# A transformer kernel on one core: output projection by token tiles, with the next norm's first tile transposed inside it

## What is computed

```python
for l in range(DEPTH):                                   # DEPTH = 2
    x = x + 0.5 * swiglu_ffn(rms_norm(x, ffn1_norm[l]), ffn1_w_in[l], ffn1_w_out[l])
    h = rms_norm(x, mix_norm[l])
    ...                                                  # three mixers y_a, y_b, y_c and gates g from h @ w_in
    merged = (g[:, :, 0] * (y_a @ w_branch[l, 0])
              + g[:, :, 1] * (y_b @ w_branch[l, 1])
              + g[:, :, 2] * (y_c @ w_branch[l, 2]))
    x = x + merged @ w_out[l]                            # the output projection, 256x1024 by 1024x1024
    x = x + 0.5 * swiglu_ffn(rms_norm(x, ffn2_norm[l]), ffn2_w_in[l], ffn2_w_out[l])
```

## Time and profile before

| | |
|---|---|
| time, median of 3 runs | 1829.95 us (1828.91 to 1839.23) |
| the profiled execution's own time | 1829.92 us |
| its span in the profile | 1828.1 us |
| mean granted clock of PE | 0.992 |
| busy share: PE, DVE, ACT, POOL | 98%, 57%, 45%, 4% |
| chain that ended last: PE, DVE, ACT, DMA | 90%, 4%, 3%, 2% |

### The profile page before, as it was taken

The page is one execution under the profiler, slowest core; times in us unless marked ns, Lnnn a source line. Parts: engine busy times, 40 slices in busy tenths (PEclk is TensorE's granted clock), DMA queues, the critical chain, the costliest instruction groups (busy, mean ns, idle before and its releaser), DMA issues.

```text
span 1828.1 us, 27099 instructions
## 1 busy us (share of the span) xinstructions
PE 1789.1 (98%) x11448; PEld 1584.1 (87%) x11448; DVE 1046.3 (57%) x1226; ACT 818.6 (45%) x885; POOL 77.6 (4%) x145
## 2 busy tenths in 40 slices
PE   8999999999999999999999999999999999999998
PEld 8998797877999899987978779998887976889996
DVE  4555356887655455553669876455666534545553
ACT  4554345552654445543555526544123123535542
POOL 0000000000000000000000001000561100000000
PEclk9999999999999999999999999999999999999999
DMA  7537255444655645372555446855254223436371
GB/s 253 184 125 282 81 165 160 156 148 138 207 180 192 213 151 184 120 286 81 165 164 159 141 138 208 186 196 207 92 162 79 72 90 115 139 122 213 126 276 58
DMA packets 194332, 293.15 MB, mean 160 GB/s; under 512 B 9298, under 2 KB 128884, under 8 KB 194244
## 3 DMA queue, kind: packets, MB, share of 16 engines
q1 hardware_dynamic: 191988, 287.72, 46.6%
q0 software_dynamic: 1936, 4.14, 2.1%
q10 hardware_dynamic: 320, 0.01, 0.0%
HBM read 289.49 MB, written 2.36 MB: 160 GB/s over the span
## 4 chain that ended last, share of the span: by engine, by line
PE 90%; DVE 4%; ACT 3%; DMA 2%; issue 1%; ACTq 0%; DVEq 0%; SPq 0%
PE acc L225 22%; PE acc L226 22%; PE acc L227 22%; PE acc L271 3%; PE acc L194 2%; PE acc L206 2%; PE acc L3030 2%; PE acc L462 1%; DMA ring<-in_ffn_w_in 1%; PE acc L2725 1%; PE acc L253 1%; PE acc L1304 1%; ACT big L1432 1%; ACT part_hi L216 1%; PE turn L1409 1%
## 5 line engine op out<-in xcount | busy, mean ns | idle before, releaser
L430 DVE TENSOR_TENSOR w_lo<-ring,w_hi 128x2048 fp32r<-128x2048 f32 x160 | 361.9, 2290 | 211.4 <-ACT w_hi L426 211.3
L225 PE MATMUL acc<-xT_hi,w_hi 128*128 128x256 f32 x1680 | 476.0, 283 | 1.2 <-DVE w_lo L430 0.8
L227 PE MATMUL acc<-xT_hi,w_lo 128*128 128x256 f32 x1680 | 475.4, 283 | 0.0
L226 PE MATMUL acc<-xT_lo,w_hi 128*128 128x256 f32 x1680 | 475.4, 283 | 0.0
L426 ACT ACTIVATE w_hi<-ring 128x2048 fp32r<-128x2048 f32 x160 | 301.3, 1912 | 150.1 <-PE acc L227 99.6
L225 PEld LDWEIGHTS acc<-xT_hi,w_hi 128*128 128x128 f32 x1680 | 322.5, 192 | 1.7 <-DVE w_lo L430 1.0
L226 PEld LDWEIGHTS acc<-xT_lo,w_hi 128*128 128x128 f32 x1680 | 322.5, 192 | 0.0
L227 PEld LDWEIGHTS acc<-xT_hi,w_lo 128*128 128x128 f32 x1680 | 322.5, 192 | 0.0
L225 PE MATMUL acc<-w_hi,hT_hi 128*128 128x512 f32 x440 | 172.3, 392 | 0.0
L227 PE MATMUL acc<-w_hi,hT_lo 128*128 128x512 f32 x440 | 171.3, 389 | 0.0
L226 PE MATMUL acc<-w_lo,hT_hi 128*128 128x512 f32 x440 | 171.3, 389 | 0.0
(11 more groups left out here) (550 smaller groups left out, 2978.7 us busy)
## 6 DMA issues: line engine op xcount, KB each, us to landing
ring<-in_ffn_w_in SPq DMA_DIRECT2D x88, 1024.0 KB, 6.1
ring<-in_w_in SPq DMA_DIRECT2D x52, 1024.0 KB, 5.0
ring<-in_ffn_w_out SPq DMA_DIRECT2D x44, 1024.0 KB, 6.4
ring<-in_w_branch SPq DMA_DIRECT2D x12, 1024.0 KB, 5.1
ring<-in_w_out SPq DMA_DIRECT2D x12, 1024.0 KB, 4.9
ring<-in_w_gate SPq DMA_DIRECT2D x11, 1024.0 KB, 5.2
ring<-in_w_up SPq DMA_DIRECT2D x11, 1024.0 KB, 6.8
ring<-in_w_down SPq DMA_DIRECT2D x11, 1024.0 KB, 6.0
```

The source lines that it names most:

```text
L225: pe.matmul(o, a_hi, wh, start=start, stop=False)
L226: pe.matmul(o, a_hi, wl, start=False, stop=False)
L227: return pe.matmul(o, a_lo, wh, start=False, stop=stop)
L430: vec.tensor_tensor(w_part(w_lo, r), raw_part(c0, r), w_part(w_hi, r).bitcast(F32), ALU.subtract).then_inc(f.lo, 1)
```

## The change

The projection's loops are exchanged: for each token tile m, for each half n, its two chunks. Tile 0 is so complete after half of the blocks. `tail.vec` of tile 1 is waited for once, ahead of its first block. Ahead of the last half (m = 1, n = 1), PE transposes tile 0 of the next norm (n2), which `first_gate` then leaves out (`turned=True`). DVE handles the transposed tile 0 before it waits for tile 1 (`late` is left out). Chunk 12 is split sooner: on ACT between the two tiles of merged, on DVE ahead of tile 1 of merged. Chunk 13 is split last as before. The chunks in the ring and the order of the loads are the same.

```diff
-        def ffn_pe(pe, f, n, c0, G0, between, asides={}):
+        def ffn_pe(pe, f, n, c0, G0, between, asides={}, turned=False):
...
-                norm_pe(pe, n, tiles=(0,))
+                if not turned:
+                    norm_pe(pe, n, tiles=(0,))
                 wait_chunk(pe, c0)
...
                 last_branch_pe(pe)
-                for n in range(2):
-                    for m in range(MT):
-                        pe.wait_ge(tail.vec, 6 + 2 * m)
+                for m in range(MT):
+                    pe.wait_ge(tail.vec, 6 + 2 * m)
+                    for n in range(2):
+                        if m == 1 and n == 1:
+                            norm_pe(pe, n2, tiles=(0,))
                         for i in range(2):
                             if n == 0 and m == 0 and i == 1:
                                 merged_pe(pe, 1)
...
                 merged_in_act(act, 0)
+                tail_part_act(act, 12)
                 merged_in_act(act, 1)
-                tail_part_act(act, 12, 13)
+                tail_part_act(act, 13)
...
                 last_branch_vec(vec, 1, 1)
-                tail_part_vec(vec, 11)
+                tail_part_vec(vec, 11, 12)
                 merged_vec(vec, 1)
                 merged_in_vec(vec, 1)
-                tail_part_vec(vec, 12, 13)
+                tail_part_vec(vec, 13)
...
                 add_norm_vec(vec, lambda e, m: add_tile_to_x(e, m, C_WO + 3, G_WO, 1.0, 3 * l + 2), n2, col[:, R["ffn2"]:R["ffn2"] + 8],
-                             late=True, between=lambda e: first_split_vec(e, f2, C_FFN2))
+                             between=lambda e: first_split_vec(e, f2, C_FFN2))
...
-                ffn_pe(pe, f2, n2, C_FFN2, G_FFN2, lambda e: None, asides={4: params2_pe, 6: s5_c_pe} if l == DEPTH - 1 else {})
+                ffn_pe(pe, f2, n2, C_FFN2, G_FFN2, lambda e: None, asides={4: params2_pe, 6: s5_c_pe} if l == DEPTH - 1 else {}, turned=True)
```

## The result

The changed kernel takes 1846.88 us (median of 12 runs, 1835.85 to 1855.51) against 1835.54 us before (12 runs, 1828.91 to 1843.73). The ratio is 1.0066, 95% interval 1.0046 to 1.0086: slower by 0.66% (11.3 us between the medians), within the 1% of the forecast's "same", but above its range and more than its 7.3 us. The profiled execution took 1841.32 us, span 1839.5 us, 11.4 us over that of before.

The account below looks back on a forecast made before the run. PE, busy 98% of the span, was taken as the bound. Per layer 2.66 + 0.99 - 0.18 + 0.17 = 3.64 us, 7.3 us for two layers on 1829.92, gave 1837.2 us; range 1831.5 to 1843.5.

Parts of the forecast that it names:

- Wait for chunk 13: At the projection's fourth block PE waits 2.38 us for this split; with a slower first matmul, +2.66 us a layer.
- Transposes in the stream: Tile 0's eight transposes, moved inside the projection, add 0.99 us a layer to PE's stream.
- The gap behind T: PE's 2.06 us wait after the projection's last block (end T) moves behind the first FFN product; only 0.18 us gained.
- FFN's chunk 1: In the second FFN, its later load and waiting ACT copy delay tile 1's square by 0.17 us (0 to 1.1).
- Chunks 12 and 0 and tile 0's transposes: Projection and FFN: all in time, costing nothing; chunk 12 by 0.9 us, chunk 0 with three blocks, transposes with 0.4 us cover.
- rival (a): PE's clock falls to half in the projection's and FFN's new waits, one to four times: 1839 to 1844 us; chance 0.28.
- (b): No wait for chunk 13 at the projection's fourth block: only 0.98 us a layer lost, 1831.9 us; chance 0.12.
- (c): Gap before the FFN really removed: 1.07 us a layer gained, 1827.8 us with no wait for chunk 13; chance 0.05.
- The 0.96 for "within 1%": Whole kernel: chance 0.96 that the time stays within 1% of before, neither faster nor slower by more.

Follow-up runs that it names:

- experiment 3: Changed kernel with the next norm's tile 0 transposed behind the last block again, leaving loop exchange and sooner chunk 12 split; ratio 1.0049 to the kernel before.
- experiment 1: Changed kernel with chunk 13 split sooner on ACT and DVE; ratio 1.0023 to the kernel before.
- experiment 2: Changed kernel with both new waits kept but filled with throwaway matmuls, five and four; ratio 1.0039 to the kernel before.
- Experiment 4: Changed kernel with chunk 13 split sooner and the second wait covered by 4 us of products ahead of tile 1's transposes; ratio 0.9989 to the kernel before.
- 5 to 8: Experiment 3 with chunk 13 sooner, 1.0009; experiment 1, second wait filled, 1.0009; kernel before, three old waits filled, 0.9979; Experiment 4, those three filled, 0.9984.

## Why the prediction was wrong

**The terms of the sum.** Wait for chunk 13: forecast 2.38 us of waiting and 2.66 in all; the changed kernel waited 2.38, experiment 3 has 2.66 and 2.64. The chain behind it (DVE two splits, copy of merged tile 1, ACT, DVE) was as told, step by step. Transposes in the stream: forecast 0.99, measured 0.94 and 1.00 (experiment 1). The gap behind T: forecast that it moves behind the first product and gives 0.18 back; B is 10.54 in experiment 2 against 10.55, so it moved and gave nothing back. Tile 1's transposes began 3.90 us behind T', the number forecast; what I had as 4.08 before was read from the chain, while the same instructions began at 466.65 = T + 3.92 by PE's own list, so the 0.18 was not there. FFN's chunk 1: forecast 0.17 of delay. It landed 5.1 us after its issue, and its copy was done at 465.78, 0.8 us before tile 1's square could start (0.7 in layer 1); nothing. Sum: forecast 3.64 a layer, measured 3.52 and 3.51 (experiment 2). Chunks 12 and 0 and tile 0's transposes were in time and cost nothing.

**The step that failed** is the one at which rival (a) was kept out of the forecast: the falls of PE's clock behind "two waits of 2.4 and 1.9 us into each layer, between these sizes" stand in the sum with nothing, and (a) got 0.28. I read the waits of 2.1 and 3.2 us as special, because transposes or long pauses stood around them, and took the 2.06 us gap behind T as the nearest row. But that gap has transposes in it and only 1.2 us of idle PE, and the row that I named for it shows the clock within the gap and not behind it (it is 1.00 there too). Both new waits, 2.4 and 2.2 us of nothing, are nearer to the other rows. Two more waits of the kernel before, of just these lengths, I left out altogether: one of 2.4 us (ended at 1331.2) and one of 1.9 us (ended at 1366.2), with windows behind them:

```profile
PE turn L2235 <- ACT big L2242: 2.4, 1, 2.4
...
PE acc L2372 <- issue: 1.9, 1, 1.9
```

```profile
1334.00:1336.00 2.00, 2.00 (x6) 1.62 (x5) 0.34 (x1) 1.43 (x2) 1.69 (x9) 0.50 0.00 0
1367.00:1370.00 3.00, 3.00 (x61) 3.00 (x61) 3.00 (x9) 0.00 (x0) 0.00 (x0) 0.50 1.05 401
```

So in that profile all five waits of 1.9 to 3.2 us were followed by a fall, and no wait of 0.9 to 1.4 us had one in the 5 us behind it (the 4.5 us ahead of the run's first matmul, at 1.00, are a case of their own). What the runs showed in place of the nothing: three falls behind the four new waits of the changed kernel's profile, at about 1.5 us each (11.98 - 10.54 = 1.44 in B, 37.43 - 35.85 = 1.58 in A), and a mean clock that puts 5 to 6 us on them, some three to four in an execution (an estimate: the 5 to 6 us are good to 4). The price in (a) was right; its place outside the sum was not: 7.3 us and three or four falls make 12 to 13, measured 11 to 12.

**The base.** The median of before that stood at the start, 1829.95, was of 3 runs; over 12 it is 1835.54, over 35 it is 1834.8. The profiled execution, on which the sum was made, was one with a clock of 0.992, and times of this kernel run from 1826 to 1842, with the clock for the most part (correlation -0.93 to -0.97). The forecast as a ratio, 1.0040, lies just under the measured interval; the upper end of the range, 1.0074, lies in it. The range was worked out in microseconds from a base 5 us too low: of the 9.7 us between 1837.2 and 1846.88, 5.6 are the base and 4.0 the change itself (11.3 against 7.3). With 1835.54 as its base the same range would have held the result, without the mechanism being any better.

**The rivals.** (b), no wait for chunk 13, is out: the wait stood there in both layers. (c), the gap really removed, is out for the change as made. Experiment 4 shows what it needed, namely 4 us of products ahead of tile 1's transposes, and that it then gains 0.3 to 0.5 us a layer, less than the 1.07 I gave it. The 0.96 for "within 1%" was right.

**Left open.** The 3.2 us wait in layer 1's second FFN was 0.8 us before, 0.6 to 1.4 in the profiles of experiments 1 to 3 and 5 to 8, and 2.4 in that of 4; the load beside POOL's parameter loads took 26.5 to 29.1 us to land. No run ties it to the change, and none excludes it. Why the clock falls behind a wait in one execution and not in the next of the same code is open too.

## What to carry to other kernels

A wait that is moved isn't removed: follow the last arrival (here tile 1's norm, 3.9 us behind the last product) and ask how much work stands ahead of its first use; 2 us of cover for a path of 3.9 leaves the gap as long as it was, and what used to be done in it is now paid extra. When a chunk is needed sooner, look at the one behind it too: its place in the queues of two engines decides, and moving one split past another's copies cost 2.7 us a layer. And price an idle PE of 2 to 3 us in the middle of dense work at its length plus, more often than not, a stretch at half clock, 1.5 us here. If the wait can't go, try to fill it: the one kernel that did only this ran at 0.9979 of before, just clear of 1. When two profiles are compared, count the falls in each first, since they come and go outside the change as well.

## What the runs showed of the hardware

I had not expected how much of the spread between runs is the clock: the kernel's times, 1826 to 1842 us, follow the mean granted clock, 0.988 to 0.996, with a correlation of -0.93 to -0.97. Waits of 2.4 us, and of 2.2 us with a product before and transposes behind, were followed by stretches at 1.2 GHz (granted clock 0.50) in some executions and layers and not in others of the same code (B 11.98 in one layer and 10.53 in the other in experiment 1), each costing about 1.5 us. Nine throwaway matmuls a layer in the two waits, 4.5 us together (five and four, 128x256 in fp32, 2.32 and 1.89 us long), were enough to hold 2.4 GHz in both layers of the profile. Not every fall has a wait ahead of it: in the profile of before the clock also went to 0.50 at 228, behind 32 matmuls of 8 columns that took 3.63 us without a pause. The Trainium skill, "TensorE: Matmul & The Clock Gate", Part 4, says that transposes don't count as a busy PE in the same way; the second wait alone, with transposes behind it, lowered the mean clock no more than the first alone, with dense matmuls behind it (0.9897 and 0.9892), so that the mean clock gives it no extra weight. In the profiles three of four such waits and one of four of the others were followed by a fall, which points the page's way but is too few to decide.
